# RWKV pairs of a hybrid decoder: the samples' state step moved from VectorE to GpSimd, beside the chunk loop

## What is computed

```python
def step(S, inp):
    r_t, w_t, k_t, v_t, kk_t, a_t = inp
    sa = jnp.einsum('bhvk,bhk->bhv', S, -kk_t)
    S = (S * w_t[:, :, None, :] + sa[..., None] * (kk_t * a_t)[:, :, None, :]
         + v_t[..., None] * k_t[:, :, None, :])
    return S, jnp.einsum('bhvk,bhk->bhv', S, r_t)
```

## Time and profile before

| | us |
|---|---|
| median of 3 runs | 4421.18 (4418.97 to 4423.82) |
| the profiled execution, its own time | 4419.04 |
| its span, first to last instruction | 4417.3 |
| TensorE busy | 3689.3 (84%) |
| VectorE busy | 1797.8 (41%) |
| GpSimd busy | 1087.7 (25%) |
| ScalarE busy | 1058.4 (24%) |

### The profile page before, as it was taken

The page is one execution under the profiler, slowest core; times in us unless marked ns, Lnnn a source line. Parts: engine busy times, 40 slices in busy tenths (PEclk is TensorE's granted clock), DMA queues, the critical chain, the costliest instruction groups (busy, mean ns, idle before and its releaser), DMA issues. The chain is left out here.

```text
span 4417.3 us, 64085 instructions
## 1 busy us (share of the span) xinstructions
PE 3689.3 (84%) x26728; PEld 3061.6 (69%) x26728; DVE 1797.8 (41%) x2022; ACT 1058.4 (24%) x1551; POOL 1087.7 (25%) x576
## 2 busy tenths in 40 slices
PE   7981567767887789999998975888888779999998
PEld 6980546656756258888877974444477469999998
DVE  2009554553233057777771003666631521111112
ACT  3112222222222021111112112555522332111111
POOL 2212301110210057777772100000011012212221
PEclk8995767777999789999999987999999989999999
DMA  3100000002220957777752113877732211111111
GB/s 115 47 28 5 4 6 7 4 4 67 80 86 20 352 176 239 245 255 244 236 196 82 34 39 139 310 281 268 283 113 67 86 34 48 44 48 48 46 46 63
DMA packets 320327, 496.65 MB, mean 112 GB/s; under 512 B 23966, under 2 KB 214699, under 8 KB 319528
## 3 DMA queue, kind: packets, MB, share of 16 engines
q1 hardware_dynamic: 204944, 423.22, 27.1%
q10 hardware_dynamic: 115096, 69.29, 5.3%
HBM read 465.80 MB, written 26.68 MB: 111 GB/s over the span
## 5 line engine op out<-in xcount | busy, mean ns | idle before, releaser
L567 POOL TENSOR_TENSOR w_lo<-w_raw,w_hi 128x1024 fp32r<-128x1024 f32 (+1 forms) x136 | 317.2, 2332 | 898.7 <-ACT w_hi L612 898.7
L419 POOL TENSOR_TENSOR w_lo<-w_raw,w_hi 128x1024 fp32r<-128x1024 f32 (+1 forms) x78 | 168.3, 2162 | 1341.6 <-ACT w_hi L397 1341.6
L718 PE MATMUL ps<-h_ffn_hi,w_hi 128*128 128x344 f32 (+1 forms) x1760 | 444.8, 350 | 11.1 <-DVE h_ffn_lo L311 7.0
L718 PE MATMUL ps<-h_ffn_lo,w_hi 128*128 128x344 f32 (+1 forms) x1760 | 442.3, 349 | 0.0
L718 PE MATMUL ps<-h_ffn_hi,w_lo 128*128 128x344 f32 (+1 forms) x1760 | 441.1, 348 | 0.0
L612 ACT ACTIVATE w_hi<-w_raw 128x1024 fp32r<-128x1024 f32 (+1 forms) x136 | 140.7, 1036 | 1206.4 <-PE ps L718 1203.0
L606 POOL TENSOR_TENSOR k_ring<-k_ring,query_rows 128x1024 f32<-128x1024 f32 x160 | 400.1, 2525 | 1.5 <-DMA k_ring<-in_cache_sb_k 1.5
L656 DVE TENSOR_REDUCE cache_logits<-k_ring 128x16 f32<-128x1024 f32 x256 | 307.8, 1220 | 136.0 <-POOL k_ring L606 132.7
L718 PEld LDWEIGHTS ps<-h_ffn_hi,w_hi 128*128 128x128 f32 x1760 | 310.2, 189 | 48.2 <-issue 10.3
L718 PEld LDWEIGHTS ps<-h_ffn_lo,w_hi 128*128 128x128 f32 x1760 | 312.0, 189 | 27.8
L718 PEld LDWEIGHTS ps<-h_ffn_hi,w_lo 128*128 128x128 f32 x1760 | 309.1, 188 | 27.8
(11 more groups left out here) (498 smaller groups left out, 6866.7 us busy)
## 6 DMA issues: line engine op xcount, KB each, us to landing
k_ring<-in_cache_sb_k SPq DMA_DIRECT2D x256, 512.0 KB, 4.4
v_ring<-in_cache_sb_v SPq DMA_DIRECT2D x256, 512.0 KB, 6.5
w_raw<-in_w_ffn_gate ACTq DMA_DIRECT2D x44, 512.0 KB, 3.9
w_raw<-in_w_ffn_up ACTq DMA_DIRECT2D x44, 512.0 KB, 3.9
w_raw<-in_w_ffn_down ACTq DMA_DIRECT2D x40, 512.0 KB, 3.5
w_raw<-in_w_in_ab SPq DMA_DIRECT2D x22, 512.0 KB, 3.8
ahead_w<-in_w_ffn_gate SPq DMA_DIRECT2D x5, 2048.0 KB, 20.3
ahead_w<-in_w_ffn_up SPq DMA_DIRECT2D x5, 2048.0 KB, 19.7
```

The source lines that it names most:

```text
L419: pool.tensor_tensor(W[m % 2].lo[:, :, :], raw[m % 2][:, :, :], W[m % 2].hi[:, :, :].bitcast(F32), ALU.subtract).then_inc(s.w_low, 1)
L567: eng.tensor_tensor(block_of(W[j % 2].lo, j), block_of(raw[j % 2], j), block_of(W[j % 2].hi, j).bitcast(F32), ALU.subtract).then_inc(s.w_l ...
L718: last = pe.matmul(ps[:, (q % slots) * nb + n, 0:w], wp, xp[:, n * w:(n + 1) * w], start=k == 0 and a == 0, stop=k == kt - 1 and a == 2)
```

## The change

The samples' step moves to GpSimd's stream, behind the masks of the last level. GpSimd makes the two fills at once and then waits for the rows. TensorE multiplies one spread row behind each of the chunks 1, 4, 6, 8 and 10, always into bank 7; the new states of even and odd chunks now share bank 6. ScalarE copies a spread row from PSUM to a new tile `r8` in SBUF two chunks later, behind its scaling of the state. GpSimd does the products and sums from SBUF. The two reductions stay on VectorE: one in chunk 7, between its sum for `u` and the new state, the other behind the loop. The diff, cut:

```diff
+        r8 = sb("sample_spread", [P, 2, NS * HD])
...
                         pool.tensor_tensor(halves(tmp, b), halves(lt, b), mask(3 + lvl), ALU.mult).then_inc(s.level_t, 1)
+                sample_step(pool, s, g, s8, t8, r8, p8, sa, vec, vs8)
...
-                dve.wait_ge(s.s8_in, 16)
-                sample_step(dve, link, s, g, ps, s8, t8, p8, sa, vec, vs8, tmp)
...
                     dve.tensor_tensor(u[rows, (c // 2) % 2, :, :], ps[rows, 4:6, 0:HD],
                                       tokm(hh)[rows, c // 2, :, :], ALU.add).then_inc(s.u_taken, 1)
+                    if c == 7:
+                        dve.wait_ge(s.sa_ready, 1)
+                        dve.tensor_reduce(sa[:, :], p8[:, :, :], AX.X, ALU.add).then_inc(s.sa_done, 1)
                     dve.wait_ge(s.s_made, c + 1)
                     dve.wait_ge(s.decayed, c + 1)
-                    dve.scalar_tensor_tensor(S[:, (c + 1) % 2, :], ps[:, 6 + c % 2, 0:HD], dend[:, c:c + 1], S[:, 2, :],
+                    dve.scalar_tensor_tensor(S[:, (c + 1) % 2, :], ps[:, 6, c % 2 * HD:(c % 2 + 1) * HD], dend[:, c:c + 1], S[:, 2, :],
                                              ALU.mult, ALU.add).then_inc(s.s_taken, 1)
+                dve.wait_ge(s.sa_ready, 2)
+                link(dve.tensor_reduce(tmp[:, T:NT], p8[:, :, :], AX.X, ALU.add))
+                dve.sem_inc(s.y8, 1)
                 dve.wait_ge(s.y_taken, 1)
...
                     act.activation(S[:, 2, :], S[:, c % 2, :], ACT.Copy, scale=dend[:, c:c + 1]).then_inc(s.decayed, 1)
+                    for n in (k for k, at in enumerate(SPREAD_AT) if at + 2 == c):
+                        act.wait_ge(s.spread_made, n + 1)
+                        if n >= 2:
+                            act.wait_ge(s.row_free if n > 2 else s.sa_ready, n - 2 if n > 2 else 1)
+                        act.activation(r8[:, n % 2, :], ps[:, 7, :], ACT.Copy).then_inc(s.spread_used, 1)
...
-                for n in range(5):
-                    pe.wait_ge(s.spread, n + 1)
-                    if n >= 2:
-                        pe.wait_ge(s.spread_used, n - 1)
-                    pe.matmul(ps[:, 6 + n % 2, :], g.blockones[:, :], t8[:, n % 2, :, :].rearrange("p b k -> p (b k)"),
-                              start=True, stop=True).then_inc(s.spread_made, 1)
-                pe.wait_ge(s.spread_used, 5)
                 pe.wait_ge(s.g_taken, 6)
...
                     last.then_inc(s.y_made, 1)
+                    for n in (k for k, at in enumerate(SPREAD_AT) if at == c):
+                        pe.wait_ge(s.spread, n + 1)
+                        if n:
+                            pe.wait_ge(s.spread_used, n)
+                        pe.matmul(ps[:, 7, :], g.blockones[:, :], t8[:, n % 2, :, :].rearrange("p b k -> p (b k)"),
+                                  start=True, stop=True).then_inc(s.spread_made, 1)
...
+SPREAD_AT = (1, 4, 6, 8, 10)
...
+    def spread(n):
+        pool.wait_ge(s.spread_used, n + 1)
+        return r8[:, n % 2, :].rearrange("p (b k) -> p b k", k=HD)
+
+    pool.wait_ge(s.vec_taken, 1)
     fill(0)
     fill(1)
+    pool.wait_ge(s.s8_in, 16)
+    link(pool.tensor_tensor(p8[:, :, :], s8[:, :, :], spread(0), ALU.mult))
+    pool.sem_inc(s.sa_ready, 1)
+    fill(2)
+    link(pool.tensor_tensor(s8[:, :, :], s8[:, :, :], spread(1), ALU.mult))
+    pool.sem_inc(s.row_free, 1)
+    fill(3)
+    pool.wait_ge(s.sa_done, 1)
+    for n, rows in ((2, sa), (3, vs8)):
+        link(pool.tensor_tensor(p8[:, :, :], spread(n), rows[:, :].unsqueeze(2).to_broadcast([P, NS, HD]), ALU.mult))
+        pool.sem_inc(s.row_free, 1)
+        link(pool.tensor_tensor(s8[:, :, :], s8[:, :, :], p8[:, :, :], ALU.add))
+        if n == 2:
+            fill(4)
+    pool.sem_inc(s.s8_done, 1)
+    link(pool.tensor_tensor(p8[:, :, :], s8[:, :, :], spread(4), ALU.mult))
+    pool.sem_inc(s.sa_ready, 1)
```

More of the change, by code:

```diff
@@ L1244, in rwkv_pair @@
                    "s8_in", "s8_done", "stored", "mean", "cent", "csq", "var", "vroot", "gsum", "rows_t", "rows_c",
-                   "decayed", "y8", "act_steps", "k_inverted", "k_spread", "v_inverted", "v_spread", "v_copied") as (s, block):
+                   "decayed", "y8", "act_steps", "pool_steps", "sa_ready", "sa_done", "row_free", "k_inverted", "k_spread", "v_inverted", "v_spread", "v_copied") as (s, block):
             @block.sync
@@ L1562, in _ @@
                     heads = [(slice(64 * h, 64 * h + 64), slice(tt * P + h * 64, tt * P + h * 64 + 64),
-                              u[cpr, ub, h, :], ps[64 * h:64 * h + 64, 6 + cp, 0:HD],
+                              u[cpr, ub, h, :], ps[64 * h:64 * h + 64, 6, cp * HD:(cp + 1) * HD],
                               ps[64 * h:64 * h + 64, c // 8, (c % 8) * C:(c % 8 + 1) * C],
@@ L1589, in _, with sample_step, link @@
                 unpack(e_prev, 4, s.v_spread)
-def sample_step(dve, link, s, g, ps, s8, t8, p8, sa, vec, vs8, y):
+SPREAD_AT = (1, 4, 6, 8, 10)
+def sample_step(pool, s, g, s8, t8, r8, p8, sa, vec, vs8):
     order = [1, 0, 2, 3, 4]
+    count = [0]
+    def link(ins):
+        count[0] += 1
+        ins.then_inc(s.pool_steps, 1)
+        pool.wait_ge(s.pool_steps, count[0])
     def fill(n):
         if n >= 2:
[L1600 to L1603, removed]
+            pool.wait_ge(s.spread_made, n - 1)
+        pool.tensor_tensor(t8[:, n % 2, :, :], g.ident2[:, :].unsqueeze(1).to_broadcast([P, NS, HD]),
+                           vec[:, order[n], :].unsqueeze(2).to_broadcast([P, NS, HD]), ALU.mult).then_inc(s.spread, 1)
@@ L1605, in spread @@
     def spread(n):
-        dve.wait_ge(s.spread_made, n + 1)
-        return ps[:, 6 + n % 2, :].rearrange("p (b k) -> p b k", k=HD)
+        pool.wait_ge(s.spread_used, n + 1)
+        return r8[:, n % 2, :].rearrange("p (b k) -> p b k", k=HD)
+    pool.wait_ge(s.vec_taken, 1)
     fill(0)
     fill(1)
[L1611 to L1632, removed]
```

## The result

| | before | after |
|---|---|---|
| median, us | 4421.3 (8 runs, 4412.69 to 4428.41) | 4408.32 (8 runs, 4403.51 to 4412.61) |
| the profiled execution, its own time | 4419.04 | 4412.56 |
| its span | 4417.3 | 4410.8 |

The ratio is 0.997, 95% interval 0.9959 to 0.9981: 13 us faster (8 to 18). The direction was right and 4408.3 lies in the range, but the forecast change of 28 us is more than twice the measured one. Rival A, the clock down in the loop, gave 4407. In this and all later ratios the kernel before was measured again on the same occasion; its medians were 4418.0 to 4421.3 us.

The account below looks back on a forecast made before the run. The loop was taken as a chain of latencies, the samples' step as a serial piece ahead of it; 10.15 + 8 × 0.33 − 3 × 1.45 − 2 × 0.80 − 0.2 = 6.6 us a turn, 26.6 in four, gave 4393 us, range 4378 to 4411.

Parts of the forecast that it names:

- Rival A: TensorE's clock stays down in the chunk loop: 3.0 us gained a turn, 12 in all, 4407 us; chance 0.27.
- Serial piece, removed: Samples' step ahead of the chunk loop goes; loop starts about 0.06 us behind the `hh` copy: 10.15 us gained a turn.
- The chunk at either clock: Each chunk of the loop gains 0.33 us at TensorE's upper clock, nothing at the lower.
- Spreads at the upper clock: Each spread matmul pair in the loop costs 1.12 − 0.32 = 0.80 us, 0.95 at worst.
- Spreads at the lower clock: Each spread matmul pair in the loop costs 1.71 − 0.26 = 1.45 us, 1.54 if only 0.17 hides.
- VectorE's reduction: In chunk 7, 0.69 us in a gap of 0.63: 0.2 us lost (0.1 to 0.7); the one behind the loop, nothing.
- ScalarE, GpSimd, SP: Copies fit ScalarE's gaps, GpSimd's fills and products finish in time, SP's later store is hidden: no cost.
- Clock: Two chunks up at first, then half; spreads raise it mid-loop for six chunks and two spreads; last chunks at half.
- Rival B: TensorE's clock stays up through the whole loop: 11.2 us gained a turn, 45 in all, 4374 us; chance 0.10.
- Rivals C and D: C: GpSimd holds VectorE up in the loop, 4439 us, chance 0.05. D: late GpSimd fill stalls TensorE, 4415, chance 0.06.
- small dependent matmuls don't hold the clock: In the loop they neither raise TensorE's clock nor, it was assumed, hold it; the loop before ran at 0.50.

Follow-up runs that it names:

- the twelve loops above: The four chunk loops each of the changed kernel (profiled execution 4412.56 us), its repeat (4391.95 us, one execution), and it without GpSimd's products and sums (median 4408.41 us).
- The loop with the addition in the kernel before: Kernel before the change, samples' step in place, plus a full-width matmul of 128 columns behind each chunk: 4448.15 us, ratio 1.0072.
- the early spreads: Changed kernel with fills ahead of GpSimd's masks and five spread matmuls moved from the loop to TensorE's wait behind the Gram blocks: 4370.64 us, ratio 0.9891.
- fill128: Changed kernel with spreads moved behind the Gram blocks, plus 128-column matmuls behind each chunk and one of 384 columns ahead of the loop: 4355.76 us, ratio 0.987.

## Why the prediction was wrong

- **Serial piece, removed: right.** The loop starts 0.25 us behind the last `hh` copy (10.22 before): 9.97 gained against 10.15. The forecast start of 0.06 us behind the copy was too early.
- **The chunk at either clock: right.** New states follow each other by 1.44 or 1.45 us at the upper clock and by 1.74 or 1.77 at the lower, 0.31 less against 0.33. (The 58 records in 1.73 us lie 0.027 us apart and not 0.030; that is within the rounding of the term.)
- **Spreads at the upper clock: right.** 0.71 against 0.80.
- **Spreads at the lower clock: mis-sized.** The step took 1.71 − 0.26 = 1.45; measured 1.76. The 0.26 that was taken to be hidden was right (566.77 to 567.01), the spread's own length was not: the two passes of 512 columns keep the next chunk from starting for 2.00 us (566.77 to 568.77), not for 1.71. The trace shows where the 0.29 lies. The second pass starts 1.01 us behind the first, and the next chunk's matmul 0.99 behind the second, where 0.853 was put for each. That figure came from the spacing inside a row of six passes; the first spacing of those six was longer too, 0.73 instead of 0.57, and the step left it out. The bound of 1.54 did not hold the cost either. This is 1.5 us a turn with five spreads at that clock.
- **VectorE's reduction: right.** The new state of chunk 7 follows `u` by 1.05 us instead of 0.88 beside it, 0.2 lost at the lower clock; at the upper, in the fourth turn, 0.3 (new states 2.48 us apart instead of 2.16). The last reduction is hidden.
- **ScalarE, GpSimd, SP: right.** No copy or fill was waited for in the loop by TensorE.
- **Clock: the failed step.** "That the spreads bring it up near the middle, for six chunks and two spreads" was a rule for every turn, and no loop followed it. Of the twelve loops above, four came back up behind the first spread and stayed (0.91), three were up near the tenth chunk or later for no more than 3 to 7 us (0.63, 0.64), and five were down from the second spread on at the latest (0.52 to 0.59). The first part of the step, some two chunks at the upper clock, was right. The forecast put a typical loop at 31.5 us and its clock between 0.6 and 0.8; those were 28.4 us, or 34 to 36.5. In the profiled execution 16 of the 20 spreads met the lower clock, where the sum had 12. A turn that stays nearly wholly down gains 38.2 − 36.8 = 1.4 us, one that is nearly wholly up 9.6. The 13 us of the medians are 3.2 a turn, between the two and near the lower end. As an estimate from these numbers, of the 11 us by which the profiled loops missed the forecast (15.4 against 26.6), some 5 are the spreads' price (16 times 0.31) and some 6 the clock.
- **Rival A** had the right total by two errors that met: it left the clock down in all turns, and priced the spreads at 1.45. With 1.76 it would have been 10.15 + 0.33 − 8.8 − 0.2 = 1.5 a turn, 6 us. The rest of the 13 comes, by this sum, from turns that were up; the executions behind the median were not profiled one by one.
- **Rival B** is real for single turns, and with added work for all. The Trainium skill's page "TensorE: Matmul & The Clock Gate", part 1, says that sustained activity releases the throttle. The loop with the addition in the kernel before, busy 35.26 of 35.26 us by its records and at 0.50, disagrees with it in its plain form; the same addition in a loop that starts at the upper clock agrees with it in that the clock holds.
- **Rivals C and D** did not occur: new states took 0.28 us beside GpSimd, and GpSimd's broadcast operands made it faster (1.04 us), not slower.
- One sentence of the prediction turned out to be the key, and was priced as a detail: small dependent matmuls don't hold the clock. With the early spreads it fell 2.2 to 4.3 us into each loop. `fill128` is that sentence taken seriously.

## What to carry to other kernels

Work that is taken off one engine's serial stretch doesn't become free if its partner instructions on another engine land in a chain of latencies: look for the place where that engine waits anyway, here 5 us behind the Gram blocks, which kept all of the gain. In a loop of small dependent matmuls read the granted clock next to the length of every repetition; where it differs between repetitions of the same code, the clock is the variable, and added wide work that fits the idle time can shorten the loop, but it did so here only in loops that started with the clock up. Where such a change is judged, a single execution says little: two of the same program differed by 20 us.

## What the runs showed of the hardware that was not expected

- The granted clock of TensorE was 1.00 through loops with one more full-width matmul of 128 columns a chunk when dense work went directly before them, and 0.50 through loops with the same addition that began at 0.50. Holding and raising are not the same.
- Adding five wide matmul pairs to each loop of the changed kernel (0.52 to 0.91, 34.1 us as a mean) gave loops that all ran at 0.88 or 0.89 and took 34.3 to 34.5 us.
- A GpSimd `tensor_tensor` of 128x512 takes 1.04 us when one operand is a column repeated over the inner 64 columns, 1.27 otherwise. On VectorE both forms take 0.69.
- A spread of two passes of 512 columns occupies TensorE for 2.00 us at the lower clock and 1.05 at the upper. At the lower clock its two spacings are 1.01 and 0.99 us, above the 0.853 which the inner spacings of six passes of 344 columns give; what fills the difference is not shown.
- Left open: what exactly decides, in the changed kernel, which turn is up. In the twelve loops the distance from the loop's first matmul to the clock's first fall orders, without exception, what the clock did up to the second spread. It was not controlled in any run, and it doesn't order the late returns of the clock in three of them.
